# Moving the normalised input and the activations to other remainders of 512 bytes, in a two-block transformer kernel

## What is computed

```python
h = rms_norm(x, gain_pre)          # normalised input
h = stage(h)                       # projection(s), a mixer or a gate, output projection
x = x + (0.5 or 1) * rms_norm(h, gain_post)
```

## Time and profile before

| | before |
|---|---|
| runs, us | 2190.2, 2192.0, 2197.65 (median 2192.0) |
| profiled execution, us | 2194.85, of which the span of the trace is 2193.1 |
| mean granted TensorE clock | 0.970 of 2.4 GHz |
| TensorE matmul busy | 2070.3 us, 94% of the span, 15066 instructions |
| weight loads busy (beside the matmuls) | 1908.6 us, 87% |
| DVE busy | 1391.7 us, 63% |
| ACT busy | 945.8 us, 43% |
| GpSimd busy | 31.9 us, 1% |
| DMA | 341.46 MB, mean 156 GB/s |

### The profile page before, as it was taken

How to read it: one execution, slowest core, us unless ns; L and a number is a source line. 1 busy time by engine, 2 the same in 40 slices (tenths; PEclk the granted TensorE clock), 3 DMA queues, 4 the chain that set the end, 5 groups by cost and what they waited for, 6 DMA issues and landing times.

```text
span 2193.1 us, 37138 instructions
## 1 busy us (share of the span) xinstructions
PE 2070.3 (94%) x15066; PEld 1908.6 (87%) x15066; DVE 1391.7 (63%) x1849; ACT 945.8 (43%) x1258; POOL 31.9 (1%) x48
## 2 busy tenths in 40 slices
PE   6989999999989999999998989999999995899998
PEld 6869988999869988997988878998899894688996
DVE  6757756655657755774666565776577456575773
ACT  4444434333444444443343243444444332544442
POOL 0000000000000000000000000000000000000000
PEclk9999999999999999999998889999999997999999
DMA  7325554443414554555530124455455543142552
GB/s 286 135 95 192 191 201 166 153 171 135 154 68 173 191 201 154 191 193 181 210 109 1 59 98 153 154 191 202 154 191 192 201 170 113 36 167 102 185 199 109
DMA packets 49788, 341.46 MB, mean 156 GB/s; under 512 B 5776, under 2 KB 6544, under 8 KB 9616
## 3 DMA queue, kind: packets, MB, share of 16 engines
q1 hardware_dynamic: 45216, 321.21, 40.8%
q10 hardware_dynamic: 4464, 18.68, 2.3%
HBM read 338.82 MB, written 1.05 MB: 155 GB/s over the span
## 4 chain that ended last, share of the span: by engine, by line
PE 82%; DVE 12%; ACT 3%; issue 2%; DMA 0%; POOL 0%; DVEq 0%; ACTq 0%; SPq 0%; POOLq 0%
PE pj L229 14%; PE pj L228 14%; PE pj L230 14%; PE acc L234 7%; PE acc L236 7%; PE acc L235 7%; DVE wlo L304 2%; PE pj L567 2%; PE pj L234 2%; PE pj L235 2%; PE pj L236 2%; PE acc L641 2%; ACT whi L297 1%; PE pj L573 1%; PE acc L628 1%
## 5 line engine op out<-in xcount | busy, mean ns | idle before, releaser
L304 DVE TENSOR_TENSOR wlo<-raw,whi 128x2048 fp32r<-128x2048 f32 x288 | 659.9, 2291 | 316.2 <-ACT whi L297 315.3
L228 PE MATMUL pj<-xh,whi 128*128 128x256 f32 x2704 | 760.8, 281 | 18.7 <-DVE wlo L314 13.5
L229 PE MATMUL pj<-xl,whi 128*128 128x256 f32 x2704 | 758.9, 281 | 0.0
L230 PE MATMUL pj<-xh,wlo 128*128 128x256 f32 x2704 | 757.3, 280 | 0.0
L297 ACT ACTIVATE whi<-raw 128x2048 fp32r<-128x2048 f32 x299 | 569.2, 1909 | 428.9 <-PE acc L236 209.0
L228 PEld LDWEIGHTS pj<-xh,whi 128*128 128x128 f32 x2704 | 510.9, 189 | 21.8 <-issue 16.0
L229 PEld LDWEIGHTS pj<-xl,whi 128*128 128x128 f32 x2704 | 510.8, 189 | 0.1
L230 PEld LDWEIGHTS pj<-xh,wlo 128*128 128x128 f32 x2704 | 509.2, 188 | 0.0
L234 PE MATMUL acc<-whi,AR 128*128 128x512 f32 x656 | 261.2, 398 | 6.7 <-DVE AR L1967 4.4
L235 PE MATMUL acc<-whi,AR 128*128 128x512 f32 x656 | 260.1, 396 | 0.0
L236 PE MATMUL acc<-wlo,AR 128*128 128x512 f32 x656 | 259.7, 396 | 0.0
(11 more groups left out here) (351 smaller groups left out, 2425.2 us busy)
## 6 DMA issues: line engine op xcount, KB each, us to landing
raw<-in_wstream SPq DMA_DIRECT2D x302, 1024.0 KB, 4.8
F<-in_gains ACTq DMA_DIRECT2D x12, 512.0 KB, 4.6
F<-in_rpb ACTq DMA_DIRECT2D x3, 1024.0 KB, 4.8
F<-in_memtok ACTq DMA_DIRECT2D x2, 1024.0 KB, 4.8
F<-in_memin ACTq DMA_DIRECT2D x2, 1024.0 KB, 6.9
F<-in_small ACTq DMA_DIRECT2D x1, 1536.0 KB, 10.6
F<-in_xin SPq DMA_DIRECT2D x2, 512.0 KB, 6.7
xt<-in_xtok SPq DMA_DIRECT2D x1, 1024.0 KB, 12.5
```

What stands on the lines that cost most here:

```text
L228: nc.tensor.matmul(o, wh, k_hi, start=first, stop=False, skip_group_check=True)
L229: nc.tensor.matmul(o, wh, k_lo, start=False, stop=False, skip_group_check=True)
L230: return nc.tensor.matmul(o, wl, k_hi, start=False, stop=last, skip_group_check=True)
L304: nc.vector.tensor_tensor(wlo[:, gs, :], raw[:, gs, :], whi[:, gs, :].bitcast(F32), ALU.subtract).then_inc(w_lo, 1)
```

## The change

No instruction is added, removed or reordered. The spacer shrinks from 112 to 96 float32 (448 to 384 bytes), and `AR` is placed at the remainder of `whi` instead of that of `xl`.

```diff
         xt = sb("xt", [P, 2, D])
         xh = sb("xh", [P, KT, T], F32R)
-        x_at = nc.sbuf_base
         xl = sb("xl", [P, KT, T], F32R)
-        sb("space", [P, 112])
+        sb("space", [P, 96])
         raw = sb("raw", [P, 3, CHUNK])
+        w_at = nc.sbuf_base
         whi = sb("whi", [P, 3, CHUNK], F32R)
...
-        ar_at = -(-(nc.sbuf_base - x_at - 0) // 512) * 512 + x_at
+        ar_at = -(-(nc.sbuf_base - w_at) // 512) * 512 + w_at
```

## The result

| | before | after |
|---|---|---|
| median of 20 runs, us | 2192.45 | 2200.31 |
| ratio after / before, 95% interval | | 1.0023 (1.0013 to 1.0033) |
| profiled execution, us (span) | 2194.85 (2193.1) | 2198.77 (2196.9) |
| mean granted TensorE clock | 0.970 | 0.969 |

The change makes the kernel slower by 0.23%, some 5 us (the means are 2193.3 and 2198.4 us; the medians lie 7.9 us apart). That is clear of the measurement's interval, though small. The 20 runs after are not spread evenly: 17 lie between 2196.1 and 2202.0 us, three at 2187.1 to 2188.4. The instructions are the same, in the same order on every engine.

What follows compares the result with a forecast made beforehand. The prediction took TensorE's matmul pace to bound the feed-forwards, with waits for DVE and ACT in the mixers. Its terms summed to 0 against the profiled 2194.85 us, so it forecast the median, 2192 us; 8-in-10 range 2150 to 2232.

Steps and rivals of the forecast that it cites:

- term 1: In tile_fm and slices_pe, x minus weights going from +64 to +128: taken as 0 us, bounds -37 to +37 us.
- term 3: In out_pe, weights minus AR going from -64 to 0: taken as 0 us, bounds -18 to +18 us.
- slower rival: In out_pe at distance 0 the two reads meet, costing 8.7 ns each, 18 us, 2210 us; chance 0.28.
- faster rival: In the feed-forwards, distance 128 favours the 113.4 ns pace and they keep it, 2155 us; chance 0.34.

Runs made afterwards that it cites:

- e1: Against the changed kernel, AR put back to 64 bytes from the weights, x left at 128; ratio to before 1.0040, median 2198.88 us.
- e2: Against the changed kernel, x put back to 64 bytes from the weights, AR left at 0; ratio to before 0.9964, median 2186.14 us.
- e5: Against the changed kernel, x and AR both moved to 448 bytes (minus 64) from the weights; 2177.4 us in one run.
- e9: Against the changed kernel, x moved to 448 bytes (minus 64) from the weights, AR left at 0; ratio to before 0.9906, median 2171.95 us.
- e10: Against the changed kernel, x moved to 192 and AR to 256 bytes from the weights; ratio to before 0.9926, median 2176.37 us.
- e3: Against the changed kernel, x and AR back at 64 bytes from the weights, everything shifted by 448 bytes; ratio to before 0.9999, median 2193.06 us.
- e8: Against the changed kernel, x moved to 64 + 512 bytes from the weights, AR left at 0; 2185.46 us in one run.
- e11: Against the changed kernel, x moved to 320 bytes from the weights, AR left at 0; ratio to before 0.9962, median 2185.99 us.

## Why the prediction was wrong

I forecast no measurable change, 2192 us, with 0.38. The measured ratio is 0.23% above 1, inside the 0.3% I called indistinguishable, but more runs than I had in mind tell it apart, and the direction is slower. More important, the reason behind the forecast was wrong: not "nothing moves" but two effects of over 10 us each against each other. That the number came out close is luck: two terms taken as 0 were each off by more than 10 us, with opposite signs.

**What held.** The frame: no instruction added, TensorE bound in the feed-forwards, the pace read from starts, DVE, ACT and loads untouched (2291 ns for L304 again, engines waited 6.9 us for the loads after, 6.2 before). The counts held, and with them the bounds of both terms: +13.3 us lies within the 37 of term 1, -10.7 within the 18 of term 3. The range holds the measured median.

**Term 1, the step that failed.** I took 0 for x's distance because tile_fm at +64 and pair_tm at -64 had the same two paces, and concluded that distance doesn't set the pace. Equal paces at two distances show only that these two are equal. With period 256 and a pace set common to +64 and -64, the trace before held no second value of the variable at all. At a third distance the pace is another: 118.8 ns at 128, 120.1 at 0. And two windows of pair_tm show which paces it has, not how often: in groups of 12 steps over the trace before, pair_tm has the quick pace in 26 of 72, tile_fm with x in 22 of 643. Alike in their paces, the two streams were not alike. The term measured +13.3 us (e1: +11.0; at the full clock and without waits 12.6 and 12.3). Of that, 6336 steps by 0.9 ns are 5.7 us in the feed-forwards, and the other 3648 by the same 0.9 ns 3.3 us. The lost stretches at 113.4 ns, which my term held for unrelated to addresses, are some 3 us: their share fell from 7 to 0.2%. Stretches at 120.0 instead of 118.8 add under 1. The term also counted the 384 matmuls of 256 columns that take AR for x, which go to distance 0 and not to 128; they are in the +0.2 us of the table's third row.

**Term 3, the same fault.** I argued from an equal loss per column in out_pe and tile_fm that the loss doesn't come from the two reads meeting. The experiments show that it does depend on the distance of those reads, so a loss proportional to columns was no evidence. It measured -10.7 us (e2: -10.8), a gain of 6.5 ns in each of the steps of out_pe.

**The slower rival** was right in the sign of the total and wrong in place and mechanism. It had the reads collide in out_pe at distance 0; that is out_pe's best distance, and the loss sits in the projections. The faster rival's pace is real, and addresses make it more or less frequent: at 192 and 448 it filled 5 of the 18 feed-forwards' projections in e5, e9 and e10, at 64 and 320 none of 30 (before, e2, e3, e8, e11), and at the 128 of the change it is gone. No address tried makes TensorE keep it.

**The two rules.** The Trainium skill (SBUF — State Buffer, "Who interferes with whom") says that PE waits on no other engine, and the trace agrees so far as it goes: DVE and ACT were as busy in windows with 90 matmuls as in those with 87. But the two independent read ports that the same section of the Trainium skill gives TensorE don't make the paces independent of where the two operands lie. Moving only their distance took the feed-forwards' projection from 117.9 to 120.1 ns (2%) and out_pe from 226.8 to 234.3 (3%).

The formula of the Trainium skill (TensorE: Matmul & The Clock Gate, "Back-to-back issue gap"), 109.2 and 215.8 ns, was reached by these streams in no run; the best were 113.4 and 226.7. The prediction used it as a floor for a stream, but the Trainium skill gives it there for a matmul by itself, and for a stream with its weight loads some 131 ns at 512 columns. No run here comes near that either.

**What stays open.** Shown is that the relative place of the stationary and the moving operand decides which paces occur, and that at the one shift tried (448 bytes) their absolute place doesn't. The period of 256 bytes is shown for x at three pairs of distances, for AR only at 0 and 256. That the read of the next stationary operand holds up the moving one inside the memory is only an argument. Why a stream has two paces at one distance and what puts it into one of them isn't known; nor why 256 and 512 columns want different distances, nor why the runs after were granted a lower clock on average than those before.

## What to carry to other kernels

In a kernel bound by back-to-back fp32r matmuls, treat the distance between stationary and moving operands as a tuning variable of its own: read the pace from starts, keep one distance per kind of stream, and try the steps of 32 or 64 bytes over one period of 256. Move one distance at a time, since a change of two can hide 13 us behind 11. Compare runs at the same granted clock: here 0.005 of it was worth some 10 us, twice the difference that was to be explained. And do not infer from equal rows at two values that a variable has no effect: ask first whether these two values could be alike by symmetry or by period.

## What the runs showed of the hardware that I had not expected

- The pace of fp32r matmuls depends on where the operands lie to each other, by a period of 256 bytes in a partition: 120.1 ns at 0 and 256 in the projection, 117.9 at 64 and 320, 118.8 at 128.
- The order of the distances is opposite for the two widths: 0 is the slowest place for 256 moving columns (120.1 ns) and the quickest for 512 (226.8 ns against 233.3).
- Some distances have two stable paces, 117.9 and 113.4 ns, and 233.3 and 228.9, held for up to 960 matmuls. The quick one took 26 to 41% of the 256-column steps with x at 192 or 448, 5 to 9% at 64 or 320, and none to speak of at 128. At 32 the second pace is 116.7 ns, at 128 it is the slower 120.0.
- DVE and ACT showed no dependence on any of these addresses: 2291 ns for L304 before, after and in the best version.
